# Two half-filled input tiles of a linear-attention layer packed into one, with the weight hand-over moved by one

## The reference

```
proj = x @ w_in
q (6 heads of 64), kv (3 branches x k,v x 2 heads of 64), 18 gate logits   # sparse attention
gq (6 x 32 = 192), gk (192), gv (384), low-rank gate (16), og (384)        # gated linear attention
pu (256)                                                                   # pooling
kc, vc = compress(k, v): gelu(windows @ cmp_w1) @ cmp_w2                   # 15 windows of 32 tokens
s_cmp = q @ kc ; p_cmp = softmax(mask(s_cmp)) ; o_cmp = p_cmp @ vc
o_slc, o_win = softmax(q @ k) @ v for two more branches, weighed by the gates
mix = concat(o_cmp + o_slc + o_win, gated linear attention, pooled) @ w_out
h = layer_norm(...) ; feed-forward ; layer_norm
```

## Time and profile before

| | |
|---|---|
| median of 3 runs | 1428.54 us (1428.52 to 1430.21) |
| span of the profiled execution | 1427.0 us |
| PE busy | 1389.4 us, 97% |
| DVE busy | 1048.1 us, 73% |
| ACT busy | 832.7 us, 58% |
| POOL busy | 531.4 us, 37% |
| DMA | 235.62 MB, mean 165 GB/s |
| layer 0, input product and attention | about 9 to 112 us of the span |
| the same in layer 1 | about 316 to 418 us of the span |

### The profile page before, as it was taken

How to read it: one execution, slowest core, us unless ns; L and a number is a source line. 1 busy time by engine, 2 the same in 40 slices (tenths; PEclk the granted TensorE clock), 3 DMA queues, 4 the chain that set the end, 5 groups by cost and what they waited for, 6 DMA issues and landing times.

```text
span 1427.0 us, 30284 instructions
## 1 busy us (share of the span) xinstructions
PE 1389.4 (97%) x12907; PEld 1175.9 (82%) x12907; DVE 1048.1 (73%) x1349; ACT 832.7 (58%) x1253; POOL 531.4 (37%) x421
## 2 busy tenths in 40 slices
PE   9999999999999999999999999999999999999997
PEld 7778888888778888878678788887888787888886
DVE  5787886566797884568687888756878865798852
ACT  6585544337575453356885656554776777566652
POOL 0144995132056991225210366501213211156610
PEclk9999999999999999999999999999999999999999
DMA  9534466544343665525336265553533333456550
GB/s 370 179 123 145 162 217 213 188 164 152 116 147 111 225 223 197 197 101 172 109 107 249 94 207 202 167 192 112 187 139 119 105 119 134 162 208 207 188 167 31
DMA packets 35863, 235.62 MB, mean 165 GB/s; under 512 B 4752, under 2 KB 6800, under 8 KB 8976
## 3 DMA queue, kind: packets, MB, share of 16 engines
q1 hardware_dynamic: 35728, 233.68, 47.7%
HBM read 232.62 MB, written 1.05 MB: 164 GB/s over the span
## 4 chain that ended last, share of the span: by engine, by line
PE 82%; DVE 11%; ACT 5%; issue 2%; DMA 0%; ACTq 0%; DVEq 0%
PE psum L694 24%; PE psum L696 24%; PE psum L695 24%; DVE low L2198 3%; PE psum L812 2%; ACT high L1582 1%; ACT m L1936 1%; PE psum L861 1%; DVE m L2655 1%; DVE arena L2658 1%; DVE arena L2316 0%; DVE u L2498 0%; DVE arena L2305 0%; PE psum L1409 0%; PE psum L1481 0%
## 5 line engine op out<-in xcount | busy, mean ns | idle before, releaser
L2198 DVE SCALAR_TENSOR_TENSOR low<-raw,high 128x2048 f16<-128x2048 f32 (+4 forms) x246 | 532.0, 2169 | 211.5 <-ACT high L1582 211.2
L694 PE MATMUL psum<-u,high 128*128 128x272 f16 (+3 forms) x2108 | 580.4, 275 | 5.5 <-DVE u L2498 4.1
L696 PE MATMUL psum<-u,low 128*128 128x272 f16 (+3 forms) x2108 | 580.0, 275 | 0.0
L695 PE MATMUL psum<-u,high 128*128 128x272 f16 (+3 forms) x2108 | 580.0, 275 | 0.0
L1582 ACT ACTIVATE high<-raw 128x2048 f16<-128x2048 f32 (+4 forms) x246 | 420.1, 1711 | 128.1 <-PE psum L696 92.3
L694 PE MATMUL psum<-arena,high 128*128 128x256 f16 (+2 forms) x1264 | 347.5, 275 | 4.6 <-issue 1.7
L695 PE MATMUL psum<-arena,high 128*128 128x256 f16 (+2 forms) x1264 | 347.5, 275 | 0.0
L696 PE MATMUL psum<-arena,low 128*128 128x256 f16 (+2 forms) x1264 | 347.4, 275 | 0.0
L694 PEld LDWEIGHTS psum<-u,high 128*128 128x128 f16 (+1 forms) x2108 | 206.5, 98 | 41.3 <-DVE u L2498 5.8
L695 PEld LDWEIGHTS psum<-u,high 128*128 128x128 f16 (+1 forms) x2108 | 206.6, 98 | 30.2 <-issue 0.7
L696 PEld LDWEIGHTS psum<-u,low 128*128 128x128 f16 (+1 forms) x2108 | 206.6, 98 | 29.6
(11 more groups left out here) (338 smaller groups left out, 1492.9 us busy)
## 6 DMA issues: line engine op xcount, KB each, us to landing
raw<-stream SPq DMA_DIRECT2D x208, 1024.0 KB, 4.8
raw<-stream SPq DMA_DIRECT2D x8, 768.0 KB, 4.2
raw<-stream SPq DMA_DIRECT2D x3, 896.0 KB, 4.8
raw<-stream SPq DMA_DIRECT2D x3, 512.0 KB, 3.5
con<-consts SPq DMA_DIRECT2D x1, 1437.0 KB, 14.2
h<-x_t SPq DMA_DIRECT2D x2, 512.0 KB, 6.3
out_t<-h SPq DMA_DIRECT2D x4, 256.0 KB, 2.1
misc<-small SPq DMA_DIRECT2D x1, 512.0 KB, 15.5
```

The lines of the kernel that those rows point to most:

```text
L694: pe.matmul(out, w_hi, x[0], start=start, stop=False)
L695: pe.matmul(out, w_hi, x[1], start=False, stop=False)
L696: return pe.matmul(out, w_lo, x[0], start=False, stop=stop)
L2198: tell(dve.scalar_tensor_tensor(low[:, at:at + w], raw[:, off:off + w], W_SCALE, high[:, at:at + w], ALU.mult, ALU.subtract), split_ready ...
```

## The change

Layers 0 and 1 only. The 64 query features and the 64 key features that were in two half-filled tiles are put in one tile, `T_GQ + 1`. The input product has 21 tiles. ACT evicts the shared tile with three instructions: the keys' half twice (rows 64 to 128 of the bank, to both halves of the place where `T_GK + 1` was), then the whole tile. Tile `one(T_GQ + 1)` goes from PE's list. The tiles behind it move up by one place in the pairs, the banks follow, and the last pair is a single tile, so its slot has 1024 columns. The pairs are now: 2 `GV, GV+1`; 3 `GV+2, KC`; 4 `KS, VC`; 5 `KW, Q`; 6 `Q+1, Q+2`; 7 `VS, VW`; 8 `PU, PU+1`; 9 `OG, OG+1`; 10 `OG+2`. Slot numbers stay as they were. On ACT and DVE the calls that make slots move, as the diff shows.

```diff
-    tiles += [run(gq0, 128), run(gq0 + 128, 64) + [None] * 64, run(gk0, 128), run(gk0 + 128, 64) + [None] * 64]
+    tiles += [run(gq0, 128), run(gq0 + 128, 64) + run(gk0 + 128, 64), run(gk0, 128), None]
-IN1_ORDER = [T_LR, T_GK, T_GK + 1, T_GQ, T_GQ + 1, T_GV, ...
+IN1_ORDER = [T_LR, T_GK, T_GQ + 1, T_GQ, T_GV, ...
-IN1_BANKS = [0, 1, 2, 3] + [0, 1, 2] * 4 + [0, 1] + [0] * 4
+IN1_BANKS = [0, 1, 2, 3] + [1, 2, 0] * 4 + [1] + [0] * 4
 # PE, first_layer
-                one(T_GQ + 1)
                 one(T_GV)
 # ACT, evac
+                    elif t == T_GQ + 1:
+                        done(first + j)
+                        tell(act.activation(p1[0:64, T_GK + 1, :], bank(BANK[first + j], 0, S, slice(64, 128)), ACT.Copy, scale=1.0 / W_SCALE))
+                        tell(act.activation(p1[64:128, T_GK + 1, :], bank(BANK[first + j], 0, S, slice(64, 128)), ACT.Copy, scale=1.0 / W_SCALE))
+                        evacuate(p1[:, t, :], first + j, S)
 # ACT, first_layer
-                for t in (T_LR, T_GK, T_GK + 1, T_GQ):
+                for t in (T_LR, T_GK, T_GQ + 1, T_GQ):
                     evac(t)
-                evac(T_GQ + 1)
                 give(0)
...
                 evac(T_KW)
+                evac(T_Q)
                 give(5)
-                evac(T_Q)
...
                 evac(T_Q + 1)
+                evac(T_Q + 2)
                 give(6)
-                evac(T_Q + 2)
                 evac(T_VS)
-                give(7)
...
                 evac(T_VW)
                 exps(0)
+                give(7)
...
                 copy_pt(0)
-                give(8)
                 exps(2)
                 copy_pt(1)
                 copy_out(0)
-                compression(0)
...
                 copy_out(2)
-                compression(1)
+                give(8)
                 exps(4)
                 copy_pt(3)
+                compression(0)
                 evac(T_OG)
                 act.wait_ge(cmp_shifted, l + 1)
                 tell(act.activation(sc[:, :, 0:CMP_N], sc[:, :, 0:CMP_N], ACT.Exp), cmp_exped)
+                compression(1)
                 give(9)
                 copy_out(3)
                 exps(5)
 # DVE, first_layer
+                weigh(3)
                 give(8)
-                weigh(3)
+                maxima(4)
                 low_part(matrices[f"cmp_{l}_0"] + SPLIT)
-                maxima(4)
-                low_part(matrices[f"cmp_{l}_1"] + SPLIT)
 
                 dve.wait_ge(cmp_scored, l + 1)
...
                 weigh(4)
                 maxima(5)
+                low_part(matrices[f"cmp_{l}_1"] + SPLIT)
                 dve.wait_ge(cmp_exped, l + 1)
```

More of the change, by code:

```diff
@@ L90 @@
 N_IN1 = 22
-IN1_ORDER = [T_LR, T_GK, T_GK + 1, T_GQ, T_GQ + 1, T_GV, T_GV + 1, T_GV + 2, T_KC, T_KS, T_VC, T_KW, T_Q, T_Q + 1, T_Q + 2, T_VS, T_VW,
+IN1_ORDER = [T_LR, T_GK, T_GQ + 1, T_GQ, T_GV, T_GV + 1, T_GV + 2, T_KC, T_KS, T_VC, T_KW, T_Q, T_Q + 1, T_Q + 2, T_VS, T_VW,
              T_PU, T_PU + 1, T_OG, T_OG + 1, T_OG + 2]
 IN1_NTH = {t: j for j, t in enumerate(IN1_ORDER)}
-IN1_BANKS = [0, 1, 2, 3] + [0, 1, 2] * 4 + [0, 1] + [0] * 4
+IN1_BANKS = [0, 1, 2, 3] + [1, 2, 0] * 4 + [1] + [0] * 4
 CMP_AFTER = 9
```

## The result

The changed kernel took 1462.0 us, the median of 4 runs (1460.67 to 1462.41). The kernel before, beside it, took 1428.59 (1428.52 to 1430.21). The ratio is 1.0226, 95% interval 1.0215 to 1.0238. The change costs 33.4 us, where 20.2 were forecast. It is slower, as forecast, but by far more than the forecast, and above its range of 1442.5 to 1454.

The account below looks back on a forecast made before the run. It took PE, 82% of the span, as the bound. Saved tile and added waits netted +8.9 us per layer, 17.8 for two; 2.4 for the clock made 20.2, so 1448.7 us, range 1442.5 to 1454.

Parts of the forecast that it names:

- The clock: Clock falls to half in the 6.1 us wait before turn(4), slowing turn(4) and OG+1: 1.2 us per layer, bounds 0 to 3.7.
- give(9): ACT's high part waits for OG+1, delaying copy_pt(4) and so values(4): 1.8 us more per layer.
- What goes: One tile per layer leaves PE: from GV on 2.61 us early; up to 1.0 may be lost in layer 0.
- give(7): On ACT between exps(0) and exps(1), it delays exps(1) by 1.80 us; PE waits 1.45 us before scores(2).
- give(8): Behind copy_out(2), its low part delays DVE's maxima(4), then copy_pt(3) and exps(4); 0.6 us in the sum before scores(5).
- compression(0): Behind copy_pt(3) on ACT, slot 13 comes late, DVE idles, weigh(4) queues; PE waits 6.1 us before turn(4).
- compression(1): On DVE behind maxima(5), its low part of 2.3 us delays the normalisation; PE waits 2.3 us before compressed_turn(0).
- Rival 2: Clock stays down through OG+1 and the steps behind it: 25.2 us in all, 1453.7 us; chance 0.10.
- rival 1: The clock holds in both layers, so the waits alone cost 17.8 us: 1446.3 us; chance 0.18.

Follow-up runs that it names:

- e1: The changed kernel with unused matmuls put into five of TensorE's waits in both layers; 1448.63 us, ratio 1.0130.
- e2: The kernel before with only give(7) moved behind exps(0) on ScalarE; 1439.47 us, ratio 1.0066.
- e11: e2 with 11 unused matmuls in the wait before scores(2); 1431.51 us, ratio 1.0015.
- e3: The changed kernel with give(7) on ScalarE moved from behind exps(0) to behind copy_pt(0); 1450.82 us, ratio 1.0147.
- e4: The changed kernel with VectorE's low part of slot 13 moved from behind maxima(4) to behind maxima(5); 1445.42 us, ratio 1.0115.
- e5: The changed kernel with give(9) on ScalarE moved from ahead of copy_out(3) to behind copy_pt(4); 1456.36 us, ratio 1.0176.
- e8: e7 with 16 unused matmuls in the wait before the state products; 1429.44 us, ratio 1.0000.
- e7: The changed kernel's packed tile kept, with a new order of hand-overs on ScalarE and VectorE; 1429.5 us, ratio 1.0000.

## Why the prediction was wrong

The direction held, and most of the mechanisms with it. The table has the start of PE's steps in layer 0, as lateness against the kernel before: as forecast without the clock's term, as measured with the clock kept up (e1), and in the change.

| step | forecast | e1 | change |
|---|---|---|---|
| `scores(2)` | -1.16 | +0.65 | +0.59 |
| `scores(5)` | -0.57 | +1.74 | +6.25 |
| `turn(4)` | +4.45 | +5.30 | +10.19 |
| `compressed_turn(0)` | +6.75 | +6.36 | +11.88 |
| `values(4)` | +8.5 | +9.32 | +16.01 |
| `values(5)` and on | +8.9 | +9.53 | +17.35 |

**The step that failed is "The clock".** It gave 1.2 us per layer with a bound of 3.7, and measured is 17.35 - 9.53 = 7.8 in layer 0. Three things in it were wrong. It took the 3.3 us between PE's last matmul and the low level at the end of the kernel as the measure, saw that in that execution the waits of 1.88 leave the clock alone (in e2 and e11 the same wait has a fall behind it in layer 0), and so asked only about the 6 us wait. The wait of 1.26 before `scores(2)` was in the sum, at 1.45, and I didn't ask what clock follows it. From `scores(2)` to `scores(4)` the change needs 91.76 - 76.50 = 15.26 us and e1 87.49 - 76.56 = 10.93, so 4.3 us went there; e3 and e2 with e11 show the same cause from both sides. And the low level was costed for `turn(4)` and `OG+1` only. `turn(4)` to `compressed_turn(0)` took 5.35 us in the change against 3.66 before, near 1.7, nearly half of the bound where a third was taken; 1.0 of it hid the wait before `compressed_turn(0)`, and the layer's lateness grew by only 0.6 there. But because give(9) waits for `OG+1`, the wait before `values(4)` grew to 4.07 and had a fall of its own behind it. The two layers together make 13.4 us where the term said 2.4. The bound of 3.7 per layer was no bound, since it covered one wait of three.

The third is the sentence "No row shows matmuls at 1.2 GHz". The trace of the kernel before has such rows, outside the two layers. PE's timeline and a window there:

```profile
1184.84 0.27 PE L694 MATMUL psum<-arena,high 128*128 128x258 f16 x1 [1.74 <-issue]
```

```profile
1186.00:1188.00 2.00, 2.00 (x11) 1.42 (x10) 0.83 (x1) 1.97 (x3) 0.00 (x0) 0.50 0.30 41
```

Behind a wait of 1.74 us the clock was low from about 1185.3 to 1188.7, and these matmuls started 0.21 us apart instead of 0.11. A wait under 2 us with a fall behind it could be read there before the change was made. It is no fixed rule: the same wait, 1.8 us in the change, left the clock at 1.00.

**"What goes" held on PE, not in layer 0's time.** 48 matmuls went. But of the 2.61 us only 56.10 - 55.36 = 0.74 were left at the states. The prediction feared this for the first hand-over, said up to 1.0, and left it out of the sum; it was 1.87. ACT's high part of slot 4 starts at 23.39 with the transfer, and PE has three new brackets of 0.33, 0.72 and 0.23 us that ACT's evictions end, while the one before the states grew by 0.29: 1.57 together, the other 0.3 is in no bracket. (PE's first product started 0.22 us earlier than before, 8.80 for 9.02, so that nearer 0.5 is unexplained.) Part of this is absorbed later, since `turn(4)` waits for DVE anyway: there e1 is 0.85 later than forecast.

**give(7)**: forecast 1.45 us of wait, measured 1.26. Right.

**give(8)**: forecast 0.6 of wait before `scores(5)`, measured 1.26. DVE's low part of 1024 columns took 1.90 and not 1.2. In e1 and e3, where the clock is up at that time, it starts at 91.1 and takes 1.28, and in e3 the wait is 0.64, as forecast. So the excess came with the low clock ahead of it. POOL is busy beside the operation in both cases (1.32 of 1.40 us in e1, 1.82 of 1.90 in the change). In e1 the low part began first and POOL's operation, which began 0.27 us later, took 1.90 us; in the change POOL's was running when it began. That the order makes the difference isn't tested.

**compression(0)**: forecast 6.1 before `turn(4)`, measured 5.07; the low part took 2.29, as said, and DVE's idle time ahead of it was 4.71, where "over 4" was forecast. Right, with PE somewhat less early than thought.

**compression(1)**: forecast 2.3 before `compressed_turn(0)`. In the change there is no bracket, since `OG+1` at half speed keeps PE busy past the release; in e1 it is 1.00. Hidden in part.

**give(9)**: the mechanism is as forecast, ACT idle before the high part of slot 15 until `OG+1` is done. The size was 1.8 and measured is 4.07 with the clock low, and in e1, behind fillers that fill 1.75 of it, another 1.15: some 2.9 with the clock up.

**The rivals.** None came. Rival 2 named the right agent, a clock that stays down behind `OG+1`, with a price of 7.4 us for both layers, which is half of the measured one, and at a place that makes the smaller part of it. The wait that did most was in no rival. e1 comes out at rival 1, the clock holding: 1446.3 by the working and 1448.6 measured. The arithmetic of waits was off by under 3 us, and some of that nearness is luck: 1.87 us of the gain was lost where the sum had nothing, and the wait behind give(9) was 1.1 longer, while the one before `compressed_turn(0)` was 1.3 shorter and `turn(4)`, which waits for DVE, took in a part of the loss. What was missing was the price of the clock behind short waits.

The Trainium skill, "TensorE: Matmul & The Clock Gate", section "Why this matters for your kernels", warns of longer idle gaps of TensorE between bursts of matmuls, and I cited it in the prediction for the long wait alone. The gaps of 5.07 and 4.07 agree with it. The gap of 1.26 before `scores(2)`, which cost most (e2 against e11), is far shorter than those of which it warns, and still the clock fell behind it (0.50 in 78 to 88); behind the gap of 1.26 before `scores(5)` it held. Here the measurement decides: a gap that the row would let pass can be the costly one.

## What to carry to other kernels

When a change adds a wait of even 1 us to the engine that bounds the kernel, price it twice: the wait, and the stretch behind it at half clock if the clock falls. If it matters which, fill the wait with unused matmuls into free PSUM and time that: the difference is the clock's share. And a tile saved on the bounding engine is worth its time only if every other engine's queue still fits in front of it; here the moves of hand-overs cost 33 us to save 5, and even the best order found gave the 5 back.

## What the runs showed of the hardware

The wait of 1.25 us before `scores(2)` was followed by 10 us or more at 1.2 GHz in the profiled execution of each of the four kernels here that have it unfilled (the change, e2, e4, e5), in both their layers. In one execution of e2 that wasn't profiled (1434.91, mean clock 0.993) it can't have come in full in both. The same wait before `scores(5)` brought no fall, in the change (1.00 in 98 to 104), and 1.12 before `turn(4)` in the kernel before brought none either. Just ahead of the wait before `scores(2)` TensorE ran the compressed branch's products, with outputs of 15 and 30 columns (73.03 to 75.24 in the change), just ahead of `scores(5)` a tile's products of 256; whether that makes the difference, no run here tests. What is shown is that without the wait (e3), or with it filled (e1, e11), the clock stays up there; the wait is needed for the fall, but not enough for one anywhere.

The wait of about 2 us before the states brought a fall in some executions and not in others of the same order: none in the change's layer 0 and one in its layer 1; none in the profiled execution of the kernel before, but one in layer 0 of e2 and of e11, whose program is the same up to there. One such fall makes PE some 1.7 us late (66.37 - 56.10 = 10.27 us from the states to `scores(0)` before, 69.78 - 57.84 = 11.94 in e2). The times of the kernel before go by such steps, near 1427.1, 1428.6 and 1430.4, with a mean granted clock of 0.998, 0.996 to 0.997 and 0.995 to 0.996. The more waits of this kind, the wider the spread can be: e4 ran from 1442.21 (clock 0.991) to 1450.76 (0.984), where the kernel before stays within 4 us. Which waits make it isn't shown: e8 fills the one before the states and is as wide as e7.

At 1.2 GHz 8 matmuls of `values` (L1094) go from 0.66 to 1.12 us and 4 of `scores` (L1061, 256 columns) from 0.70 to 1.22, from the rows of e1 and the change, 1.7 times as long; matmuls of 258 columns start 0.21 us apart instead of 0.11, nearly twice. PE's busy share (96%) hides it.
